# Fourteen output-gate blocks as seven seven-product pairs, and denominators that are not inverted

## The reference

```python
proj = xn @ w_in                                  # 2048 -> 3 * 4096
x_m, o_pre, z = split(proj)
x_c = silu(causal_conv(x_m)); q, k from x_c, v from x_m
w   = exp(dmat - m_t) * (q @ k.T)                 # causal
num = w @ v;  den = sum(w)
h   = num / maximum(abs(den), exp(-m_t))
h   = h * sigmoid(o_pre)                          # the output gate
h   = h * rsqrt(mean(h * h) + EPS) * head_norm    # over the 512 values of the head
y   = (h + skip * x_c) * silu(z) @ w_out
```

## Time and profile before

| | |
|---|---|
| median of 3 runs | 2862.31 us (2861.88 to 2862.43) |
| span of the profiled execution | 2859.2 us |
| between the two | 3.1 us |
| busy: PE / DVE / ACT / POOL | 2808.1 / 2114.6 / 1341.9 / 278.6 us |
| granted TensorE clock | nine tenths or more of full in all forty slices |
| HBM | 353.87 MB read, 74.53 MB written |

### The profile page before, as it was taken

How to read it: one execution, slowest core, us unless ns; L and a number is a source line. 1 busy time by engine, 2 the same in 40 slices (tenths; PEclk the granted TensorE clock), 3 DMA queues, 4 the chain that set the end, 5 groups by cost and what they waited for, 6 DMA issues and landing times.

```text
span 2859.2 us, 55731 instructions
## 1 busy us (share of the span) xinstructions
PE 2808.1 (98%) x21931; PEld 2729.2 (95%) x21931; DVE 2114.6 (74%) x2897; ACT 1341.9 (47%) x1763; POOL 278.6 (10%) x375
## 2 busy tenths in 40 slices
PE   7999999999999999999999999999999999999998
PEld 7899999999999999999999999999999999999898
DVE  7999999996664666665668889877775776776654
ACT  5444444445553444343343444633334555555544
POOL 0000000000000112211110100100000000000243
PEclk9999999999999999999999999999999999999999
DMA  5344444446554444544345544543333222232444
GB/s 178 131 150 141 141 148 141 140 152 247 212 192 173 166 156 164 164 164 167 115 165 177 193 139 158 202 141 127 134 119 134 89 100 96 89 100 96 165 177 174
DMA packets 99160, 430.12 MB, mean 150 GB/s; under 512 B 12224, under 2 KB 13888, under 8 KB 76640
## 3 DMA queue, kind: packets, MB, share of 16 engines
q1 hardware_dynamic: 66048, 290.57, 29.0%
q0 software_dynamic: 32496, 135.65, 14.0%
q10 hardware_dynamic: 496, 2.24, 0.2%
HBM read 353.87 MB, written 74.53 MB: 150 GB/s over the span
## 4 chain that ended last, share of the span: by engine, by line
PE 85%; DVE 5%; issue 2%; DMA 2%; ACT 1%; POOL 0%; SPq 0%; DVEq 0%; ACTq 0%; POOLq 0%
PE mm L2654 19%; PE mm L2704 14%; PE mm L2780 10%; PE ax L2780 7%; PE ax L2654 6%; PE mm L3085 6%; PE ax L3085 4%; PE ax L2876 4%; PE ax L2932 3%; PE mm L3050 3%; PE ax L3050 2%; PE mm L3027 2%; PE ax L3027 2%; PE mm L2797 1%; PE ax L3119 1%
## 5 line engine op out<-in xcount | busy, mean ns | idle before, releaser
L2654 PE MATMUL mm<-xh,w_hi 128*128 128x264 f32 (+2 forms) x1376 | 370.2, 314 | 3.7 <-DVE xl L1594 1.9
L2654 PE MATMUL mm<-xl,w_hi 128*128 128x264 f32 (+2 forms) x1376 | 366.8, 311 | 2.0 <-DVE w_lo L1582 1.9
L2704 PE MATMUL mm<-xq,w_hi 128*128 128x264 f32 x2112 | 345.7, 285 | 0.0
L2654 PE MATMUL mm<-xh,w_lo 128*128 128x264 f32 (+2 forms) x1264 | 345.6, 308 | 0.0
L1582 DVE TENSOR_TENSOR w_lo<-w_raw,w_hi 128x2048 fp32r<-128x2048 f32 x119 | 272.4, 2289 | 75.8 <-ACT w_hi L890 75.3
L2704 PEld LDWEIGHTS mm<-xq,w_hi 128*128 128x128 f32 x2112 | 293.5, 189 | 0.5
L890 ACT ACTIVATE w_hi<-w_raw 128x2048 fp32r<-128x2048 f32 x119 | 227.7, 1914 | 106.5 <-PE mm L2654 82.8
L2654 PEld LDWEIGHTS mm<-xh,w_hi 128*128 128x128 f32 x1376 | 237.7, 188 | 17.7 <-DVE xl L1594 2.4
L2780 PE MATMUL mm<-s,w_hi 128*128 128x264 f32 x1344 | 246.5, 284 | 2.1 <-DVE w_lo L1614 2.1
L2654 PEld LDWEIGHTS mm<-xl,w_hi 128*128 128x128 f32 x1376 | 234.8, 188 | 13.5 <-issue 2.4
L2654 PEld LDWEIGHTS mm<-xh,w_lo 128*128 128x128 f32 x1264 | 220.5, 189 | 12.5
(11 more groups left out here) (480 smaller groups left out, 7500.1 us busy)
## 6 DMA issues: line engine op xcount, KB each, us to landing
w_raw<-in_slots_dram SPq DMA_DIRECT2D x240, 512.0 KB, 3.5
w_raw<-in_weights_dram SPq DMA_DIRECT2D x118, 1024.0 KB, 4.8
xm_scratch<-pad POOLq DMA_DIRECT2D x32, 264.0 KB, 3.1
xc_whole<-xc_scratch SPq DMA_DIRECT2D x8, 1056.0 KB, 7.0
xm_whole<-xm_scratch SPq DMA_DIRECT2D x8, 1056.0 KB, 4.9
qk_scratch<-qkv POOLq DMA_DIRECT2D x8, 1056.0 KB, 11.7
qk_whole<-qk_scratch POOLq DMA_DIRECT2D x8, 1056.0 KB, 5.4
xc_load<-xc_scratch POOLq DMA_DIRECT2D x32, 264.0 KB, 3.6
```

The source lines that it names most:

```text
L2654: i = pe.matmul(ps[:, at:at + n], w, v[:, t0:t0 + n], start=first and k == 0, stop=last and k == 2)
L2704: i = pe.matmul(ps[:, t * BANK:t * BANK + HT], w[par_][:, k * P:(k + 1) * P], QUARTERS[t][k // HK][x][:, k % HK, :], start=k == 0 and a == ...
```

## The change

1. **Seven more pairs.** The output-gate tiles 0 and 1 of heads 1 to 7 are made as pairs 28 to 34 behind the others, ScalarE takes their tanh there (`pair_o`, `tanh_o`), and they go to a new scratch (`og_d`). SyncE stores them. In the loop head h makes two blocks in place of four; GpSimd loads the two stored tiles (`load_gates`) for head h+1 into the buffer that still holds head h-1's tiles, once all four of these are stored.
2. **No reciprocal.** The gated product is (1 + tanh) times the product, in one VectorE instruction a tile (`gated_pv`). The denominator enters the norm: ScalarE squares it (`square_dn`, scaled by 4 x 512 x EPS), VectorE adds it to the sum of squares (`norm_sum`), and `inv_norm` starts from there. The floor's exponent is capped once in the gate section (`LOG_MOST`).
3. **Order.** The denominators' product stands right in front of the values product. Its two column ranges are 16 and 512 wide, so a product is 14 matmuls in place of 20 (denominators: 10 in place of 14). The block between sum of squares and scores is gone, and the scores wait for `norm_sum`. VectorE finishes tiles of head h-1 near the end of head h.

```diff
@@ TensorE @@
             def head_a2(h):
-                pe.wait_ge(ot_ready, h * CT)
-                block_a(b + 1, 1, mm[1])
+                b = h * OWN + (A2_0 + 3)
+                pe.wait_ge(ot_ready, h * OWN + 2)
+                block_a(b, 1, mm[1])
                 sum_g(h - 1)
-                pe.wait_ge(ot_ready, h * CT + 1)
-                block_a(b + 2, 0, mm[0])
                 for j in range(3):
                     scores_a2(h, j)
-                pe.wait_ge(ot_ready, h * CT + 2)
-                block_a(b + 3, 1, mm[1])
+                pe.wait_ge(ot_ready, h * OWN + 3)
+                block_a(b + 1, 0, mm[0], range(0, 8))
                 for j in range(3, NS):
                     scores_a2(h, j)
-                pe.wait_ge(ot_ready, h * CT + 3)
-                block_a(b + 4, 0, mm[0], range(0, 10))
+                block_a(b + 1, 0, mm[0], range(8, KT))
                 den_sum(h)
-                block_a(b + 4, 0, mm[0], range(10, KT))
                 probs_v2(h)
...
                 if j == 0:
-                        pe.wait_ge(rstd_ready, h)
+                        pe.wait_ge(dn_ready, h * 4)
...
@@ VectorE @@
+            def norm_sum(h):
+                dve.wait_ge(sumg_done, h + 1)
+                dve.wait_ge(dn_ready, h * 4 + 3)
+                dve.tensor_tensor(two(dn[:, :]), halves(ax[0]), two(dn[:, :]), ALU.add).then_inc(dn_ready, 1)
...
             def head_a2(h, hp):
+                exponents(h)
                 low_qk(h)
-                exponents(h)
                 causal_w(h)
-                low_w(h * CT + (A2_0 + 3), 1)
-                tiles_y(h - 1, 1 - hp)
+                low_w(h * OWN + (A2_0 + 4), 0)
+                low_v(h)
+                norm_sum(h - 1)
                 attend(h, hp)
...
-                dve.reciprocal(dn[:, :], dn[:, :]).then_inc(dn_ready, 1)
...
+                dve.tensor_tensor(dn[:, :], ax[1][:, X0:X0 + T], dn[:, :], ALU.max).then_inc(dn_ready, 1)
+                if not first:
+                    tile_y(h - 1, 1 - hp, 2)
+                gated_pv(h, hp, 0)
+                if not first:
+                    tile_y(h - 1, 1 - hp, 3)
+                for c in range(1, CT):
+                    gated_pv(h, hp, c)
...
@@ GpSimd @@
-                    tiles_y(h - 1, 1 - hp)
                 if not (isinstance(h, int) and h == AH - 1):
                     pool.wait_ge(sc_done, h * NS + NS)
                     load_qk(h + 1)
+                if not first:
+                    tiles_y(h - 1, 1 - hp, range(CT))
+                if not (isinstance(h, int) and h == AH - 1):
+                    if not first:
+                        for i in range(2):
+                            pool.wait_ge(y_stored[i], h * 32)
+                    load_gates(h + 1, 1 - hp)
                     pool.wait_ge(pv_done, h * (1 + CT) + (1 + CT))
                     load_v(h + 1)
                     load_floor(h + 1)
...
@@ ScalarE @@
-                o_gate(h, hp, 1, mm[1])
-                inv_norm(h - 1)
                 round_v(h)
-                o_gate(h, hp, 2, mm[0])
+                o_gate(h, hp, 3, mm[1])
                 for j in range(3):
                     round_w2(h, j)
-                o_gate(h, hp, 3, mm[1])
+                inv_norm(h - 1)
                 for j in range(3, NS):
                     round_w2(h, j)
+                square_dn(h)
...
-                    o_gate(h + 1, 1 - hp, 0, mm[0])
+                    o_gate(h + 1, 1 - hp, 2, mm[0])
```

More of the change, by code:

```diff
@@ L460, in load_head @@
                     sp.wait_ge(qkv_mm, h * (2 * QT + CT) - CT)
[L461 to L465, removed]
+                    for i in range(2):
+                        sp.wait_ge(res_stored[i], h * 64 + 32)
                     load_x(h, xcr, xc_d, xcr_loaded)
@@ L507, in _ @@
                 pair(n, n)
-            with sp.Fori(1, PAIRS // 4 - 1) as i:
+            with sp.Fori(1, CZ // 4) as i:
                 for c in range(4):
                     pair(i * 4 + c, c)
-            for c in range(4):
-                pair(PAIRS - 4 + c, c)
+            for c in range(O_PAIRS):
+                pair(CZ + c, c)
             load_head(0)
@@ L677, in sum_squares_a2, with tiles_y @@
                                        ALU.add).then_inc(ss2_ready, 1)
-            def tiles_y(h, hp, last=False):
-                for c in range(CT):
+            def tiles_y(h, hp, tiles, last=False):
+                for c in tiles:
                     pool.wait_ge(y_ready, h * CT + (c + 1))
@@ L793, in _ @@
             sum_squares_a2(AH - 1)
[L794 removed]
+            tiles_y(AH - 1, (AH - 1) % 2, range(CT), True)
             for i in range(2):
@@ L1037, in _ @@
                 pair(n, n, n // 2)
-            with act.Fori(1, PAIRS // 4 - 1) as i:
+            with act.Fori(1, CZ // 4) as i:
                 for c in range(4):
                     pair(i * 4 + c, c, i * 2 + c // 2)
-            for c in range(4):
-                pair(PAIRS - 4 + c, c, (PAIRS - 4 + c) // 2)
+            pair(CZ, 0, CZ // 2)
+            for n in range(CZ + 1, PAIRS):
+                pair_o(n)
             NJ = 2 * QT + CT
@@ L1751, in pair @@
                 early = isinstance(n, int) and n < 2
+                gated = isinstance(n, int) and n > CZ
+                stored = 16 * (CZ // 2 + 2) if gated else n * 8 + 24
                 if early:
@@ L1754, in pair @@
                 else:
-                    jobs = [(n - 1, half + 1 if c % 2 == 0 else None, 2 - c % 2 * 2)]
+                    jobs = [(n - 1, half + 1 if c % 2 == 0 and not gated else None, 2 - c % 2 * 2)]
                 job_n, x, pc = jobs[0]
@@ L1778, in pair @@
                 low_slot(n, c, 6)
-                finish_tile(job_n, x, 1, pc)
+                if not gated:
+                    finish_tile(job_n, x, 1, pc)
                 if early:
@@ L1805, in pair @@
                     t_sum(n + 1, c + 1, False)
-                if not early:
+                if not early and not gated:
                     finish_tile(job_n, x, 0, pc)
@@ L1824, in _ @@
                 pair(n, n, n // 2)
-            with dve.Fori(1, PAIRS // 4 - 1) as i:
+            with dve.Fori(1, CZ // 4) as i:
                 for c in range(4):
                     pair(i * 4 + c, c, i * 2 + c // 2)
-            for c in range(4):
-                pair(PAIRS - 4 + c, c, (PAIRS - 4 + c) // 2)
+            for n in range(CZ, PAIRS):
+                pair(n, n % 4, n // 2)
             NJ = 2 * QT + CT
@@ L2785, in _ @@
                 pair(n, n)
-            with pe.Fori(1, PAIRS // 4) as i:
+            with pe.Fori(1, CZ // 4) as i:
                 for c in range(4):
                     pair(i * 4 + c, c)
+            for n in range(CZ, PAIRS):
+                pair(n, n % 4)
             NJ = 2 * QT + CT
@@ L3308, in _pack @@
         slots += [pair[0][:, 0], pair[1][:, 0], pair[0][:, 1], pair[1][:, 1]]
+    for h in range(1, ah):
+        c0 = ai + h * dv
+        pair = [m.reshape(p, 2, hk * p) for m in _blocks(a_in, d, [c0, c0 + p])]
+        slots += [pair[0][:, 0], pair[1][:, 0], pair[0][:, 1], pair[1][:, 1]]
     for f in range(ai // d):
```

224 lines of the change are left out of this document (120 added, 104 removed).

## The result

The changed kernel takes 2916.32 us (median of 4 runs, 2915.30 to 2918.80) where the kernel before takes 2862.10: ratio 1.0192, 95% interval 1.0178 to 1.0207, or +54 us. The direction and the place were forecast. The size was not: +41.7 was, and the measured time by its ratio (2862.3 x 1.0192 = 2917.3) lies just past the range's upper end of 2917.

What follows compares the result with a forecast made beforehand. The prediction took TensorE, busy in 98% of the span, to bound the kernel. Pairs +142.1, heads 1 to 7 -99.0, head 0 -0.8, junction -1.0 and exponent cap +0.4 gave +41.7: 2904 us, range 2882 to 2917.

Steps and rivals of the forecast that it cites:

- Pairs: Pair stretch: seven more pairs at 20.3 us each, at TensorE's pace, +142.1 us.
- junction: Between pairs and q, k, v: the last tile's convolution leaves VectorE's queue, -1 us, bounds 0 and -3.
- head 0: Attention loop: head 0 keeps its blocks and wins 4 x 0.16 + 0.17, -0.8 us.
- The wait: Before the first score tile: TensorE waits for VectorE's sum, 5.1 us in head 1, 7.8 in heads 2 to 7.
- The clock: Score tiles behind the wait: TensorE returns at granted clock 0.50, 1.7 us in each of seven heads.
- working time of a head: Attention loop: TensorE's own work in a new head, 40.1 us, including denominators 1.8 and values product 8.7.
- the isolated gap: Products with merged columns: skill's formula makes the merge save nothing, total some 6 us higher; the forecast used the row instead.
- The 3.1 us "between the two": Whole kernel: 3.1 us outside the span, added to the forecast span to give the forecast time.
- Faster: Rival, attention loop: VectorE reaches the sum in time, wait 0.9, clock stays up, total 2846.5; chance 0.06.
- The clock stays up: Rival, score tiles: the clock stays up through the waits, 7 x 1.7 less, 2892; chance 0.12.
- The stores are no hindrance: Rival, between heads: y stores never delay GpSimd, all heads like head 1, 6 x 2.7 less, 2888; chance 0.13.
- The stores hold longer: Rival: stores cost 2 us a head more, or new pairs 1.5 a pair more, 2914 to 2916; chance 0.10.

Runs made afterwards that it cites:

- e1: Changed kernel with VectorE taking norm_sum ahead of the low parts of v and behind everything else; 2894.15 us, ratio 1.0112 to the kernel before.
- e2: Changed kernel with VectorE taking norm_sum right behind the low parts of q and k; 2865.25 us, ratio 1.0007 to the kernel before.
- e4: Changed kernel with GpSimd's wait for y stores and its gate loads moved behind its additions of squares; 2905.26 us, ratio 1.0149 to the kernel before.
- e3c: Changed kernel with 56 unused matmuls of 264 columns filling the wait before the scores; 2903.50 us, ratio 1.0150 to the kernel before.
- e3: Changed kernel with 60 unused matmuls of 128 columns, ones by ones, filling the wait before the scores; 2912.36 us, ratio 1.0179 to the kernel before.

## Why the prediction was right or wrong

**Pairs, junction, head 0.** Right: 140.9 for 140.7. (Head 0 itself won 0.3 and not 0.8.)

**The wait.** Right in place, cause and order of size: 5.74 us in head 1 (5.1 predicted) and 8.08 on average in heads 2 to 7 (7.8). e1 and e2 show that it shrinks by what is taken out of VectorE's queue ahead of the sum, instruction for instruction. e4 shows that GpSimd's wait for the y stores is 11 us of it. The sum took 0.4 off for joints between VectorE's instructions, and there was nothing to take off: from the low parts of q and k to the sum's end they take 9.3 us in head 1 as in the rows of head 2 above. In head 1 they also start 0.2 later than in the earlier trace rows: a v load took 1.53 us to issue there, which a first addition of 1.34 in place of 2.14 didn't quite make up. In heads 2, 3, 5 and 7 the wait was 7.7 to 7.9, as forecast; in heads 4 and 6 it was 8.56, and there the gate load was issued 3.9 us behind the head's first matmul and not 2.8 to 2.9. Head 4, whose first matmul is at 1278.84:

```profile
1282.72 0.53 POOL L669 DMA_DIRECT2D ot<-og_scratch  x1 [3.76 <-DMA y_scratch<-ot]
```

Over seven heads the term was 2.3 too low, and another 1.1 for the ends of the sums of squares, which I took 0.16 earlier than the idle time is counted from.

**The clock.** Right in kind: e3c gives 13.7 us, 1.7 a head makes 11.9. The term of 1.7 a head was 2.4 us too low over seven: the score tiles took 41.4 in all, against 7 x 5.58.

**The step that failed** is the working time of a head, "8.7" for the values product and "1.8" for the denominators, which had no bounds. The second layer's product of 13 matmuls was the wrong row to scale from: 2.17 was taken, and the product takes 2.24 without waits. With the waits the four take 1175.49 - 1165.37 = 10.12 us in head 1, not 9.7, of which 4 x 0.07 is work and the rest time lost around the two waits, and the denominators 1.87, not 1.8. Over seven heads this is 3.2 us.

It is not the only term that was too low, nor clearly the largest. The loop's 9.8 us of error are 2.3 and 1.1 in the wait, 2.4 in the clock, 3.2 here, and 0.8 in pieces: score tiles 3 and 4 take 1.33 where 1.3 was put, and in heads 4 and 6 the block ahead of the sum of squares takes 11.9. Inside the loop no link of the mechanism was missing; the sizes were all off the same way. The time by its ratio lies 0.3 us past the range's end, so that any one of these terms put right would have kept it inside. I had taken the lower or middle value at each, and let the range's upper end stand on one of them being off, not on all.

By the rule of the Trainium skill that the prediction weighed (TensorE: Matmul & The Clock Gate, Back-to-back issue gap, the isolated gap) merging column ranges is worth nearly nothing, and its estimate of a total some 6 us higher was nearer on the total. But its mechanism does not hold here: a product of 4368 columns takes 2.24 us with 14 matmuls and 2.44 with 20 in the same layout, where that formula gives an estimate of 1.86 and 1.87. The merge is worth 0.09 against the layout of before (2.33), a little over half of what I took.

**Outside the loop** the trace of the changed kernel is 4.5 us longer from the output projection on (1392.6 against 1388.1). I had 0 there. 2.0 of it is scatter, by the second trace of before. The other 2.5 is there in all the variants' traces too (1392.3 at least), in TensorE's waits for low parts of weights around the norms between and behind the layers (7.3 us at one line in the changed kernel, 3.6 and 4.0 in the two traces of before), at places that differ from trace to trace (one of 2.75 us in the changed kernel where before has 1.16). What makes them longer no run shows; it stays open.

The 3.1 us "between the two", put down to the program's start and end, is in part the same scatter: in every timed run on record the time is 1.5 to 1.6 us above its span. So the profiled execution of before was itself some 1.6 us below the median, and that is most of why the spans differ by 56.3 us and the times by 54.

**The rivals.** "Faster" had the right condition: the sum taken in time. e2 gets there from VectorE's order alone and is level with before; its 2846 needed the cover too. "The clock stays up" did not happen; e3c, which kept it up, shows its price, 12.8 us where the rival has 12. "The stores are no hindrance" falls with e4, where their wait taken away gave 11 us. "The stores hold longer" came true in heads 4 and 6 alone, by 1 us each.

## What to carry to other kernels

When independent work is taken out between a producer and its consumer, read the consumer's new input back through every engine's queue: the wait that appears is the sum of what stands in front of it, and the place of one instruction in a queue can be worth as much as the change (51 us here, in e2). A long wait also costs the clock behind it (13.7 us here), on top of its own length. In a loop that closes over several engines a wait may be what keeps another chain early: take it away last, or together with the wait that the chain ends in.

## What the runs showed of the hardware

- A wait's own length did not decide whether the clock fell. It stayed at full through 2.71 us behind a whole block (e1, head 1), through 1.5 to 2.2 us behind a block in six heads of e2, and through 0.9 to 1.8 behind 56 matmuls of 264 columns in six heads of e3c. It fell with 1.1 to 1.9 us of wait behind 60 matmuls of 128 columns of ones in six heads of e3, where the engine had also been issuing without a pause. Whether the columns, the values or the moment of the wait made the difference, the runs don't separate.
- Once fallen, it was 0.50 for some 3 to 6 us of work, behind a wait of 1.25 as behind one of 7.75: score tiles of 24 matmuls took 5.2 to 6.6 us in the changed kernel for 3.88.
- A matmul of 128 columns took 0.114 us in a row of 60 (6.84 us), one of 264 columns 0.123: halving the columns saved some 8% of the time.
